# Gate and up groups with three seven-product pairs instead of two, double sums by accumulating transfers

## The reference, cut to what matters

```python
x = x + 0.5 * _swiglu(_rmsnorm(x, ffn1_norm), ffn1_w_gate, ffn1_w_up, ffn1_w_down)
u = _rmsnorm(x, mix_norm) @ w_in            # two kinds of attention, then
x = x + concat(a_out, b_out) @ w_out
x = x + 0.5 * _swiglu(_rmsnorm(x, ffn2_norm), ffn2_w_gate, ffn2_w_up, ffn2_w_down)
x = _rmsnorm(x, final_norm)
# _swiglu(x, g, u, d) = (silu(x @ g) * (x @ u)) @ d ; gate and up are 2048 x 5632
```

## Time and profile before

| | us |
|---|---|
| median of 3 runs | 1813.33 (1812.99 to 1813.91) |
| the profiled execution | 1813.86 |
| its span in the trace | 1812.1 |
| PE busy | 1800.3 (99%) |
| DVE busy | 1412.1 (78%) |
| ACT busy | 962.1 (53%) |

### The profile page before, as it was taken

One profiled execution on the slowest core, in us unless ns is written; L12 is line 12 of the kernel. 1 busy time (PEld: TensorE's weight loads), 2 busy tenths in 40 slices (PEclk: granted clock), 3 DMA queues, 4 the chain that ended last, 5 costly groups with the idle time before them and its releaser, 6 DMA issues.

```text
span 1812.1 us, 22169 instructions
## 1 busy us (share of the span) xinstructions
PE 1800.3 (99%) x8296; PEld 1500.2 (83%) x8296; DVE 1412.1 (78%) x1665; ACT 962.1 (53%) x1190; POOL 21.5 (1%) x19
## 2 busy tenths in 40 slices
PE   9999999999999999999999999999999999999998
PEld 7888888888888888888888888888888888888887
DVE  7889898889898868666666566889887887678865
ACT  7555445555455546555656445555445555345554
POOL 0000000000000000100000000000000000000000
PEclk9999999999999999999999999999999999999999
DMA  9565655555666657655464466665655557566653
GB/s 334 202 220 201 212 194 192 201 199 199 213 213 225 223 171 245 196 175 169 155 193 162 160 224 223 203 219 197 216 191 193 202 197 258 190 205 224 218 173 114
DMA packets 234115, 367.01 MB, mean 203 GB/s; under 512 B 16560, under 2 KB 95152, under 8 KB 234032
## 3 DMA queue, kind: packets, MB, share of 16 engines
q1 hardware_dynamic: 233120, 364.44, 59.2%
q10 hardware_dynamic: 912, 1.48, 0.2%
HBM read 346.85 MB, written 2.10 MB: 193 GB/s over the span
## 4 chain that ended last, share of the span: by engine, by line
PE 99%; DVE 0%; DMA 0%; issue 0%; ACT 0%; POOL 0%; DVEq 0%; SPq 0%
PE psum L1927 72%; PE psum L1968 14%; PE psum L1840 7%; PE psum L1845 3%; PE psum L1949 1%; PE psum L2117 0%; PE psum L2128 0%; PE psum L2163 0%; PE psum L2143 0%; DVE x_res L1789 0%; DMA w_raw<-in_ffn_gate 0%; PE psum L1807 0%; PE psum L1805 0%; PE psum L1806 0%; PE psum L1899 0%; PE psum L2176 0%
## 5 line engine op out<-in xcount | busy, mean ns | idle before, releaser
L1927 PE MATMUL psum<-w_split,x_split 128*128 128x512 f32 x3792 | 872.9, 390 | 0.0
L1927 PEld LDWEIGHTS psum<-w_split,x_split 128*128 128x128 f32 x3792 | 710.4, 188 | 149.0 <-DVE w_split L1252 1.4
L755 ACT ACTIVATE w_split<-w_raw 128x1024 fp32r<-128x1024 f32 (+1 forms) x520 | 518.6, 1013 | 457.7 <-PE psum L1927 326.7
L1252 DVE TENSOR_TENSOR w_split<-w_raw,w_split 128x1024 fp32r<-128x1024 f32 (+1 forms) x520 | 586.4, 1163 | 95.4 <-ACT w_split L755 89.9
L1927 PE MATMUL psum<-w_split,h_planes 128*128 128x512 f32 x1920 | 439.1, 390 | 0.0
L1927 PEld LDWEIGHTS psum<-w_split,h_planes 128*128 128x128 f32 x1920 | 360.0, 188 | 75.4 <-DVE w_split L1252 1.3
L1102 DVE TENSOR_TENSOR w_split<-w_raw,w_split 128x1024 fp32r<-128x1024 f32 (+1 forms) x244 | 284.0, 1190 | 94.2 <-ACT w_split L645 92.4
L645 ACT ACTIVATE w_split<-w_raw 128x1024 fp32r<-128x1024 f32 (+1 forms) x244 | 247.1, 1032 | 207.2 <-PE psum L1927 158.6
L1968 PE MATMUL psum<-w_split,pair_sums 128*128 128x512 f32 x624 | 162.7, 390 | 0.0
L1968 PEld LDWEIGHTS psum<-w_split,pair_sums 128*128 128x128 f32 x624 | 117.2, 188 | 24.2
L1968 PE MATMUL psum<-w_split,x_split 128*128 128x512 f32 x360 | 94.8, 390 | 0.0
(11 more groups left out here) (240 smaller groups left out, 1046.9 us busy)
## 6 DMA issues: line engine op xcount, KB each, us to landing
w_raw<-in_ffn_up SPq DMA_DIRECT2D x67, 1024.0 KB, 5.4
w_raw<-in_ffn_gate SPq DMA_DIRECT2D x66, 1024.0 KB, 7.9
w_raw<-in_ffn_down SPq DMA_DIRECT2D x64, 1024.0 KB, 5.7
w_raw<-in_w_in SPq DMA_DIRECT2D x48, 512.0 KB, 4.8
w_raw<-in_w_in SPq DMA_DIRECT2D x24, 1024.0 KB, 5.2
w_raw<-in_ffn_gate SPq DMA_DIRECT2D x42, 512.0 KB, 5.5
w_raw<-in_ffn_up SPq DMA_DIRECT2D x40, 512.0 KB, 5.8
w_raw<-in_w_out SPq DMA_DIRECT2D x16, 1024.0 KB, 5.1
```

The costliest lines, as they stand in the source:

```text
L755: nc.scalar.activation(w_split[:, n % 2, 0, part[0]:part[1]], w_raw[:, slot, part[0]:part[1]], ACT.Copy).then_inc(hi_made, 1)
L1252: nc.vector.tensor_tensor(w_split[:, n % 2, 1, part], w_raw[:, slot, part], w_split[:, n % 2, 0, part].bitcast(F32), ALU.subtract).then_in ...
L1927: ins = mm(psum[:, bank + t, :], x[:, a, t * P:(t + 1) * P], w[:, b, k, :], start=kk == from_ and (a, b) == (0, 0) and t in begins, stop=k ...
```

## The change

A group now has 11 jobs, numbered 0 to 10 here: two plain for gate, a blocks job (pair of k-blocks 12, 13), a mixed job (k-blocks 8 and 9 of gate and of up, 24 matmuls), two blocks jobs (pairs 14 and 10), a plain one for up, the three sums jobs, a plain one for up. It takes 4 x 24 + 24 + 3 x 21 = 183 matmuls and not 6 x 24 + 2 x 21 = 186. The first two sums of a pair are no longer made by DVE: POOL issues a transfer that reads two blocks of up once more and adds them onto the raw slot (`accum_op=ALU.add`), when the blocks job has been split. DVE does the two additions that depend on each other, three jobs after the blocks job was split. Three raw slots of four hold a pair until its sums job is split, so the chunks' slots are given by a table, and chunk 6 is loaded behind the mixed job. The final gate additions come behind job 9, in which the last sums are multiplied, and silu is made in the last loop step. The moved hidden of the group before is split at loop step 3 (it was at steps 7 and 8). The x side of the third pair is built in the entry group. Two loops over groups are written out, and `prepare` (tables for attention) goes from behind phase 1 to phase 5.

```diff
-SEVEN_PAIRS = (12, 14)
-SEVEN_JOBS = (("plain", 0), ("plain", 1), ("blocks", 2), ("blocks", 3), ("plain", 4), ("sums", 2), ("sums", 3),
...
+GROUP_PAIRS = (12, 14, 10)
+GROUP_JOBS = (("plain", 0), ("plain", 1), ("blocks", 2), ("mixed", 3), ("blocks", 4), ("blocks", 5), ("plain", 6), ("sums", 2),
+              ("sums", 4), ("sums", 5), ("plain", 7), ("plain", 8), ("plain", 9))
+GROUP_FREED_BY = (-4, -3, -2, -1, 0, 1, 3, 6)
+SUMMED_BY_TRANSFERS = (0, 1, 2)
+GROUP_SUMS_AT = tuple((3, 5, 6)[m] if m in SUMMED_BY_TRANSFERS else (1, 3, 6)[m] for m in range(3))
...
+                    pool.wait_ge(lo_made, lo_value(seven_base(ph, i) + GROUP_JOBS.index(("blocks", raw))))
+                    nc.gpsimd.dma_start(blocks[:, 0:4:2, :], source(i, 4 + k // 4)[:, k % 4:k % 4 + 2, :],
+                                        accum_op=ALU.add).then_inc(block_sums[m], 16)
...
-                for n in range(10):
-                    seven_high(ph, i, n + 2, ph["next_kn"] if at_end and n >= 8 else ph["kn"], silu if n == 7 else None)
+                for n in range(11):
+                    seven_high(ph, i, n + 2, ph["next_kn"] if at_end and n >= 9 else ph["kn"], silu if n == 10 else None)
...
-                    if n in (0, 2):
-                        sum_blocks(ph, i, n // 2)
-                    if n == 6:
+                    for m in range(3):
+                        if n == GROUP_SUMS_AT[m]:
+                            sum_blocks(ph, i, m)
+                    if n == 7:
+                        first_gate(ph, i)
+                    if n == 9:
                         seven_gates(ph, i)
-                    if n == 8 and not at_first:
+                    if n == 3 and not at_first:
                         moved_low(i - 1, g - 1)
```

More of the change, by code:

```diff
@@ L82, in hybrid_layer @@
     phases = []
-    s = g = r = part_at = moved_at = extra = sevens = builds = wide_steps = gates = 0
+    s = g = r = part_at = moved_at = extra = sevens = builds = wide_steps = gates = sums = 0
+    group_sums_steps = sum(2 if m in SUMMED_BY_TRANSFERS else 3 for m in range(3))
+    places = [0, 1, 2, 3]
     ff_parts = []
@@ L94, in plan_ffn @@
                            "all_moved": part < 2, "extra": extra, "sevens": sevens, "plain": int(part == 0), "gates": gates,
-                           "build": builds, "h_build": None})
+                           "build": builds, "built": builds + (3 if part == 0 else 0), "h_build": None, "sums": sums, "places": []})
+            if part == 0:
+                builds += 3
+            for i in range(n // 2):
+                phases[-1]["places"].append(places)
+                if i or part:
+                    places = [places[k] for k in GROUP_NEXT_PLACES]
+            phases[-1]["places"].append(places)
+            sevens_here = n // 2 - (part == 0)
             s, g = s + 2 * n, g + n // 2
-            extra, sevens = extra + 2 * (n // 2 - (part == 0)), sevens + n // 2 - (part == 0)
-            gates += n // 2 - (part == 0)
+            extra, sevens = extra + 3 * sevens_here, sevens + sevens_here
+            gates, sums = gates + sevens_here, sums + group_sums_steps * sevens_here
             part_at, moved_at = part_at + (part == 2), moved_at + n // 2 - (part == 2)
@@ L466, in seven_chunks @@
[L466 to L477, removed]
+                        after_wide = j == 0 and i == 0 and ph["after"]["kind"] == "seven_wide"
@@ L655, in hi_parts @@
                     act.wait_ge(used, used_value(c - 2))
-                    hi_part(c, slot, kn, h)
+                    hi_part(w_raw[:, ph["places"][0][slot], :], split_at(c) if split is None else split, kn, h)
             def copy_lo(s, j, factor):
@@ L807, in body @@
                             ins.then_inc(silu_done, 1)
-                loop(act, ph["bodies"], body, first=True, last=ph["kn"] != ph["next_kn"] or ph["h_build"] is not None)
+                for i in range(ph["bodies"]):
+                    body(i)
             def seven_wide(ph):
@@ L1260, in sum_blocks @@
[L1260 removed]
+                if by_transfer(ph, m):
+                    dve.wait_ge(block_sums[m], 16 * (group_count(ph, i) + 1))
+                else:
+                    dve.wait_ge(lo_made, lo_value(seven_base(ph, i) + jobs_of(ph).index(("blocks", raw))))
+                    nc.vector.tensor_tensor(b[:, 0:4:2, :], b[:, 0:4:3, :], b[:, 2:3, :].broadcast_to([P, 2, 2 * STRIP]), ALU.add).then_inc(weight_sums, 1)
+                    done += 1
+                    dve.wait_ge(weight_sums, done)
@@ L1394, in body @@
                             fold_sum(0)
-                loop(dve, ph["bodies"], body, first=True, last=True)
+                for i in range(ph["bodies"]):
+                    body(i)
             def seven_wide(ph):
@@ L1911, in x_turn, with wide_chunk @@
                 ins.then_inc(x_turned, 1)
-            def wide_chunk(c, slot, bank, quarter, left=None, count=KB, waits=None, during=None, begins=(0, 1), ends=(0, 1), from_=0):
-                w = w_split[:, slot % 2, :, :].rearrange("p l (k n) -> p l k n", n=2 * STRIP)
+            def wide_chunk(c, bank, quarter, left=None, count=KB, waits=None, during=None, begins=(0, 1), ends=(0, 1), from_=0):
+                w = w_split[:, split_at(c), :, :].rearrange("p l (k n) -> p l k n", n=2 * STRIP)
                 for k in range(4):
```

358 lines of the change are left out of this document (219 added, 139 removed).

## The result

The changed kernel takes 1982.12 us (median of 4 runs, 1981.43 to 1983.17) where the kernel before takes 1813.3 (4 runs, 1812.99 to 1813.91). The ratio is 1.093, with a 95% interval of 1.091 to 1.095. It is slower, as forecast, but 86 us beyond the forecast and 37 beyond the range.

What follows compares the result with a forecast made beforehand. PE bound the kernel by its number of matmuls, with DVE's reserve deciding the change. 1813.9 + 51 + 8 + 11 (groups of three kinds) + 10 (chunk 6) + 2 (entry) = 1896 us; range 1868 to 1945.

Steps and rivals of the forecast that it cites:

- the walk: Step-by-step timing of a middle group in the new order: lags of 3.9 us, +3.2 us a group, so 45.4 us.
- place 1: Ahead of job 6: PE 1.1 us late, set by DVE's row of work and by chunk 6's landing.
- The entry's third x side: Entry group: 2.5 us of DVE work hidden under plain jobs; uncovered, 5 us over both FFNs.
- Rival 4: Accumulating transfers take over 12 us and DVE waits at all three places; at 16 us, 1976; 12%.
- rivals 1 and 2: First: no new pause, 1800.3, 4%. Second: half of it hidden, about 1875; with all reserves near 1813, 2%.
- It is not free for chunk 6, though ... I take 0.6: Added transfer slows chunk 6 ahead of job 6 by 0 to 2.6 us; 0.6 taken, 10 us over 16 groups.
- rival 3: Chunk 6, loaded for job 6, is much slower, 2.6 us more a group: 1928 us in all; 15%.
- three pauses of about 4 us, silu ahead of the down phases: Last groups ahead of three down phases: DVE also builds two x sides, 3 x 3.8 = 11 us.

Runs made afterwards that it cites:

- the spare matmuls: The changed kernel with 16 extra useless matmuls ahead of job 6 in the groups that have the pause; 1951.9 us, ratio 1.076 to the kernel before.

## Why the prediction was wrong

**Direction and places: right.** PE pauses stand where the walk put them: 16 at job 6, ahead of the sums jobs, ahead of each group for silu. At place 1 the row of DVE alone leaves 0.94 us (1.1 in the walk; chunk 6 issued by ACT); job 9 had 0.65 (1.1) and silu 1.09 (1.5). The entry's third x side was hidden: the plain groups' splits cost PE 0.6 us in the whole kernel. The accumulating transfers took 6.3 us in the median, inside the 6 to 8 taken, and DVE never waited for one. Rival 4 didn't happen, and rivals 1 and 2 were far off.

**The step that failed** is "It is not free for chunk 6, though ... I take 0.6". The mechanism stood there, with its upper bound of 2.6 us (rival 3, 15%), and I took the value by the size of the added transfer. Measured is 2.3 us in the median, 2.1 to 3.5 in 15 of 16 groups. SP's moves, taken at 10.0 us, took 10.8, so that chunk 6 was issued 16.8 to 17.6 us after the group's start in 14 of them and not at 15.8 to 16.3; here the prediction had no term for POOL's transfers at all. All sums by DVE shows both back near their old values (5.4 and 10.3). Place 1 thus came to 71.4 us where 27 were counted. The excess is 44 us; the other places returned some 17, since all waits of PE together are 122 us and the walk had 95 (16 x 3.9 + 4 x 2.7 + 3 x 3.8, and 10).

The Trainium skill (DMA: Bandwidth & Descriptors, Issuing engines are not separate DMA queues), which the prediction weighed, says that transfers of all issuing engines interleave on the same DMA engines. The runs agree, 5.41 us alone and 6.67 beside a plain transfer, and the accumulating one costs more than its bytes.

**What was missing altogether** is PE's clock, and the restart. The prediction read tenths of 9 everywhere and priced a pause at its length. Behind the 15 pauses of 4.2 us or more ahead of job 6 the job took 7.3 to 8.5 us, where it takes 5.75 behind a short one, and the window shows the 1.2 GHz level. Two of silu's three pauses of 3.6 us did the same (13.6 and 13.7 us for 48 matmuls, not 11.2), and the one of 6.4 us. Together these 18 falls make 38 us of longer rows, 31 of them ahead of job 6 (15 at 2.1 on average); the spare matmuls won back 30 us of time. To this come the 0.35 us that each of the 56 pauses costs beyond its row (20 us).

The miss adds up: 27 us of waits, 38 of low clock and 20 of restarts are 85, and the profiled execution lies 86 above 1896. Rival 3 had the landing nearly right, and its 1928 is still 54 us low. Most of it hangs on place 1: 44 us of waits and 31 of low clock behind them.

The Trainium skill (TensorE: Matmul & The Clock Gate, HAM oscillation — how this bites in real kernels) describes this case: a loop that waits for a transfer in each turn restarts each turn at the low clock. The trace agrees, in 15 of the 16 groups with a pause at job 6. The prediction doesn't weigh it. Pauses of 1.1 us, as the walk had them, show no fall in the groups. But the walk also had three pauses of about 4 us, silu ahead of the down phases, and two of these show it.

## What to carry to other kernels

In this kernel, where PE never waited, a pause costs more than its length. In one like it, add the restart and, if the pause may grow to a few microseconds, the matmuls behind it at half the clock. Before adding a transfer beside one that the critical engine waits for, find the slack of that one; where it has none, issue it first (here 14 us after the group's start and not 17, behind nothing), and put helper work into holes of the timeline rather than ahead of a wait. And set the work saved (0.68 us a group here) against the smallest pause that the new order makes (silu alone, 1.1 us) before anything else.

## What the runs showed of the hardware

- A transfer of 512 KB that POOL issues took 6.3 us with accumulation and 4.5 without (medians of 60).
- POOL's accumulating transfers slow SP's issue of its own: sixteen small transfers took 10.3 us (median of 16 groups; 10.0 to 11.2) without them, also beside plain ones, and 10.8 (10.5 to 11.5) beside them.
- A 1 MB load took 5.4 us (5.2 to 5.6) with no transfer of POOL issued just before it, 6.6 (5.8 to 7.5) beside a plain one of 512 KB, and 7.7 (7.5 to 8.9) beside an accumulating one issued 0.5 to 1.7 us before it. In the one group where the accumulating one went out less than 0.1 us before it, the load took 5.95, and 5.98 in the same group of the kernel with spare matmuls (0.2 us). Why was not looked into.
- The clock's fall is no fixed matter of a pause's length. In the groups of these nine kernels it fell behind every pause of 4.1 us or more and behind none under 1.75. In between it fell in some groups and not in others: all sums by DVE has 15 pauses of 2.20 us ahead of job 6 and slow matmuls behind one of them (7.35 us, against 5.74), and the changed kernel has one of 3.60 us with none behind it. What decides there was not settled.
